# Conformer and S5 hybrid block on eight cores: first loads, DRAM casts and the convolution's steps reordered

## The reference

```python
def reference(x, meta, norm_g, w_in, b_gate, ...):
    h = jnp.concatenate([broadcast(meta), x], axis=1)     # 16 + 2048 tokens
    xn = _rmsnorm(h, norm_g)
    proj = jnp.einsum("bld,de->ble", xn, w_in)            # 2048 -> 9216
    v_c, g_c, z_c, u_s, z_s, gl_c, gl_s = _split_columns(proj)
    # mixer A: v * sigmoid(g), causal depthwise convolution of 31 taps, layernorm, silu, * silu(z)
    y_c = _conformer_conv(v_c, g_c, z_c, dw_w, dw_b, ln_g, ln_b)
    # mixer B: S5 state space scan, gelu, GLU, * silu(z)
    y_s = _s5_scan(u_s, ...)
    y_s = jax.nn.gelu(y_s)
    y_s = y_s * jax.nn.sigmoid(jnp.einsum("ble,ef->blf", y_s, w_glu) + b_glu)
    y_s = y_s * jax.nn.silu(z_s)
    merged = (jax.nn.sigmoid(gl_c + b_gate[:D_MODEL]) * jnp.einsum("ble,ed->bld", y_c, w_conv)
              + jax.nn.sigmoid(gl_s + b_gate[D_MODEL:]) * jnp.einsum("ble,ed->bld", y_s, w_ssm))
    h = h + jnp.einsum("bld,de->ble", merged, w_out)
    return _rmsnorm(h, final_g)[:, N_META:, :]
```

## Time and profile before

| | us |
|---|---|
| three timed runs, median (lowest to highest) | 1804.61 (1802.98 to 1807.88) |
| the profiled execution, its own time | 1794.7 |
| its span on the slowest core, core 5 | 1793.2 |
| spans of the eight cores | 1785.0 to 1793.2 |
| TensorE busy in that span | 1653.3 (92%) |
| VectorE, ScalarE, GpSimd busy | 738.0, 495.4, 60.9 |
| mean granted TensorE clock, all cores | 0.975 to 0.976 of 2.4 GHz |

### The profile page before, as it was taken

The page is one execution under the profiler, slowest core; times in us unless marked ns, Lnnn a source line. Parts: engine busy times, 40 slices in busy tenths (PEclk is TensorE's granted clock), DMA queues, the critical chain, the costliest instruction groups (busy, mean ns, idle before and its releaser), DMA issues.

```text
span 1793.2 us, 22788 instructions; the slowest of 8 cores (1785.0 to 1793.2 us)
## 1 busy us (share of the span) xinstructions
PE 1653.3 (92%) x8966; PEld 803.4 (45%) x8966; DVE 738.0 (41%) x1142; ACT 495.4 (28%) x700; POOL 60.9 (3%) x131
## 2 busy tenths in 40 slices
PE   1799899999999997188899999999999999999997
PEld 1344455555554443044455454444444444444443
DVE  2554488887730000245573601111221236733343
ACT  2644477777731110000131251111111100011111
POOL 1000000000000300000000000000000000000000
PEclk9999999999999999598999999999999999999999
DMA  9461022232347499700204230302221144364333
GB/s 212 143 162 42 9 72 64 70 64 67 72 96 139 58 111 111 85 16 10 33 1 71 36 60 12 59 0 40 49 51 39 46 160 165 122 229 160 141 141 117
DMA packets 33177, 149.61 MB, mean 83 GB/s; under 512 B 3936, under 2 KB 7136, under 8 KB 23648
## 3 DMA queue, kind: packets, MB, share of 16 engines
q0 software_dynamic: 13744, 60.30, 22.4%
q1 hardware_dynamic: 19328, 87.86, 13.9%
HBM read 179.07 MB, written 40.89 MB: 123 GB/s over the span
## 4 chain that ended last, share of the span: by engine, by line
PE 85%; DVE 5%; another core or an unknown queue 4%; DMA 2%; issue 2%; ACT 1%; POOL 0%; DVEq 0%; ACTq 0%; SPq 0%; POOLq 0%
PE ps L254 83%; DMA xt<-x 2%; PE ps L257 2%; DVE wc L232 1%; ACT cs L226 1%; DVE mt L232 1%; DVE xs L242 1%; DVE cs L242 0%; DVE ug L248 0%; ACT xs L228 0%; DVE g L232 0%; DVE ss L760 0%; DVE pq L232 0%; DVE ag L248 0%
## 5 line engine op out<-in xcount | busy, mean ns | idle before, releaser
L254 PE MATMUL ps<-xm,wr 128*128 128x512 bf16 x1280 | 297.4, 379 | 0.0
L254 PE MATMUL ps<-wb,xm 128*128 128x512 bf16 x1024 | 229.8, 386 | 48.9 <-DVE a L242 48.9
L254 PE MATMUL ps<-xm,zr 128*128 128x512 bf16 x1024 | 223.3, 379 | 0.0
L254 PE MATMUL ps<-wo,m 128*128 128x512 bf16 x1024 | 221.2, 379 | 0.0
L254 PEld LDWEIGHTS ps<-wb,xm 128*128 128x128 bf16 x1024 | 101.0, 100 | 172.4 <-issue 59.0
L254 PEld LDWEIGHTS ps<-xm,wr 128*128 128x128 bf16 x1280 | 119.5, 98 | 122.6 <-issue 0.2
L254 PE MATMUL ps<-xm,gr 128*128 128x512 bf16 x768 | 169.7, 379 | 0.0
L254 PEld LDWEIGHTS ps<-wo,m 128*128 128x128 bf16 x1024 | 100.2, 98 | 120.8
L254 PEld LDWEIGHTS ps<-xm,zr 128*128 128x128 bf16 x1024 | 99.6, 98 | 117.5
L254 PE MATMUL ps<-wu,xm 128*128 128x512 bf16 x512 | 120.5, 395 | 4.6 <-ACT wv L226 4.6
L228 ACT ACTIVATE jk<-h 128x2048 bf16<-128x2048 f32 x16 | 30.6, 1912 | 326.9 <-DVE h L242 326.9
(11 more groups left out here) (163 smaller groups left out, 1652.5 us busy)
## 6 DMA issues: line engine op xcount, KB each, us to landing
x<-x SPq DMA_DIRECT2D x16, 1024.0 KB, 6.9
out<-h SPq DMA_DIRECT2D x16, 1024.0 KB, 4.7
xt<-x SPq DMA_DIRECT2D x14, 1024.0 KB, 7.2
wr<-wm POOLq DMA_DIRECT2D x20, 512.0 KB, 8.6
gscr<-gst SPq DMA_DIRECT2D x20, 512.0 KB, 7.9
gr<-gscr SPq DMA_DIRECT2D x20, 512.0 KB, 3.4
wob<-wo POOLq DMA_DIRECT2D x8, 1024.0 KB, 58.6
zr<-wm POOLq DMA_DIRECT2D x16, 512.0 KB, 5.9
```

What stands on the lines that cost most here:

```text
L254: return S.op("pe", lambda e: e.matmul(out_, lhsT, rhs, start=start, stop=stop), r, w, signal=signal)
```

## The change

Six edits, in the order of the program.

**First loads.** Tiles 1 and 2 of x move from POOL's to SP's queue, tile 1 behind a wait for tile 0's landing, tile 2 behind a wait for `gf`'s. The second half of `wu` waits on POOL for tile 2's landing. `prm` moves behind them.

**Input order.** From A(i), B(i-3), T(i+2) with the norm three tiles ahead, to a written list: T0, N2, A0, T1, N3, A1 and so on, B from after T4 on. The parameter steps start at A3 instead of A1. The first scan tables are moved by a unit or two (`prep_wv(0)` before `tab_b` and `tab_c`).

**G2.** `prep_g2(q)` moves from st = 3 of q - 1 to st = 1 of q.

**DRAM casts.** The 28 casts become single instructions on POOL, each waiting for the PE unit ahead of it: seven in g1 (after units 3, 5, ... 15), eight each in v0 and v1 (odd units), five in the z part. The ten `wmb` of `wss` come first, then `wob`, then `wmb` of `wcv`. `load_wtc(0)` and `load_wtc(1)` now stand behind seven casts, not behind 28.

**Convolution.** The two copies from PSUM to `ag` go from DVE to ACT. `build_wc` is split in its two halves. `conv_tr(b + 1, 0)` moves ahead of `conv_mm(b, 1)`, `conv_tr(b, 1)` to the start of the block.

**Fillers.** One generator over all, and four places in a block instead of three: four units in each of blocks 0 to 2, eight in block 3, sixteen in blocks 4 and 5, eight in 6 and 7.

```diff
-            elif i in (1, 2):
-                dma("pool", XT[sl].ap, x_t[t], dsrc(), w=(XTb[sl],))
...
+            return dma("sp", XT[sl].ap, x_t[t], XTs[sl], w=(XTb[sl],), after=after)
...
-        load_x(0)
-        dma("sp", GF.ap, norm_g.partition_broadcast(128), dsrc(), w=(GFb,))
+        ev_x0 = load_x(0)
+        ev_gf = dma("sp", GF.ap, norm_g.partition_broadcast(128), dsrc(), w=(GFb,))
+        load_wu(0)
+        load_x(1, (ev_x0,))
+        ev_x2 = load_x(2, (ev_gf,))
         dma("sp", PRM.ap, prm_d, dsrc(), w=(PRMb,))
-        load_wu(0)
-        load_x(1)
-        load_x(2)
-        load_wu(1)
+        load_wu(1, (ev_x2,))
...
+        order = ["T0", "N2", "A0", "T1", "N3", "A1", "T2", "N4", "A2", "T3", "N5", "A3", "T4", "N6", "B0", "T5", "N7",
+                 "A4", "B1"]
+        for i in range(6, NSEQ):
+            order += [f"T{i}"] + ([f"N{i + 2}"] if i + 2 < NSEQ else []) + [f"A{i - 1}", f"B{i - 4}"]
...
-                if st == 1 and nx:
-                    tab_b(q + 1)
-                    prep_wv(q + 1)
+                if st == 1:
+                    if nx:
+                        tab_b(q + 1)
+                        prep_wv(q + 1)
+                    prep_g2(q)
...
                 if st == 3:
-                    if nx:
-                        prep_g2(q + 1)
...
+        casts = [("w", 0, i) for i in range(10)] + [("o", n, h) for n in range(4) for h in range(2)]
+        casts += [("w", 1, i) for i in range(10)]
...
+                if nb == 1 and j >= 3 and j % 2 == 1:
+                    cast((S.eng["pe"]["src"], S.eng["pe"]["src"].count))
...
-            cp("dve", AG[sl].ap[:, :, 2:130], pT.rearrange("p (g c) -> p g c", g=8), r=(PB[bk],), a=(AGb[sl],))
+            cp("act", AG[sl].ap[:, :, 2:130], pT.rearrange("p (g c) -> p g c", g=8), r=(PB[bk],), a=(AGb[sl],))
...
-            if j == 2:
-                build_wc(0)
+            if j in (2, 6):
+                build_wc(0, j // 6)
...
+        conv_tr(0, 0)
+
+        def conv_block(b, n1, n2, n3, n4):
+            conv_tr(b, 1)
             fillg(n1)
-            conv_tr(b, 1)
             conv_mm(b, 0)
+            build_wc(b + 2, 0)
             fillg(n2)
+            if b < 7:
+                conv_tr(b + 1, 0)
+            fillg(n3)
             conv_mm(b, 1)
-            fillg(n3)
-            build_wc(b + 2)
+            build_wc(b + 2, 1)
+            fillg(n4)
 
         for b in range(4):
-            conv_block(b, 1, 1, 2 if b < 3 else 1)
-        fillg(16)
-        load_z(0)
-        load_z(1)
-        gen = fill_3b()
+            if b < 3:
+                conv_block(b, 1, 1, 1, 1)
+            else:
+                conv_block(b, 2, 2, 2, 2)
         for b in range(4, 6):
-            conv_block(b, 5, 5, 6)
+            conv_block(b, 4, 4, 4, 4)
...
-            conv_block(b, 3, 2, 3)
+            conv_block(b, 2, 2, 2, 2)
```

More of the change, by code:

```diff
@@ L80, in touch, with op @@
         self.live.append(b)
-    def op(self, eng, fn, r=(), w=(), a=(), signal=True, src=None):
+    def op(self, eng, fn, r=(), w=(), a=(), signal=True, src=None, after=()):
         En = self.eng[eng]
@@ L100, in op @@
             _mx(need, b.p)
+        for ds, v in after:
+            if need.get(ds, 0) < v:
+                need[ds] = v
         kn = En["known"]
@@ L257, in tr, with dma @@
             return S.op("pe", lambda e: e.transpose(out_, in_, idn), r, w, signal=signal)
-        def dma(q, out_, in_, src, r=(), w=(), a=()):
-            return S.op(q, lambda e: e.dma_start(out=out_, in_=in_), r, w, a, src=src)
+        def dma(q, out_, in_, src, r=(), w=(), a=(), after=()):
+            return S.op(q, lambda e: e.dma_start(out=out_, in_=in_), r, w, a, src=src, after=after)
         coff = [CONST0]
@@ L338, in build, with load_x @@
         NSEQ = len(seq)
-        def load_x(i):
+        def load_x(i, after=()):
             if i >= NSEQ:
-                return
+                return None
             t = seq[i]
@@ L797, in build @@
         norm(0)
+        load_x(3)
         norm(1)
[L799 removed]
         load_x(4)
[L801 to L840 removed]
+        order = ["T0", "N2", "A0", "T1", "N3", "A1", "T2", "N4", "A2", "T3", "N5", "A3", "T4", "N6", "B0", "T5", "N7",
+                 "A4", "B1"]
@@ new lines, in build @@
+        for i in range(6, NSEQ):
+            order += [f"T{i}"] + ([f"N{i + 2}"] if i + 2 < NSEQ else []) + [f"A{i - 1}", f"B{i - 4}"]
+        order += [f"A{NSEQ - 1}"] + [f"B{i}" for i in range(NSEQ - 4, NSEQ)]
+        n_a = 0
+        for o in order:
+            i = int(o[1:])
+            if o[0] == "N":
+                norm(i)
+                load_x(i + 3)
+            elif o[0] == "T":
+                trans(i)
+            elif o[0] == "A":
+                n_a = i
+                uproj(i, 0)
+                if i >= 3:
+                    next(par, None)
+                    next(par, None)
+                if i == 10:
+                    for i_ in range(4):
+                        load_gate_w(i_)
+                if i == 14:
+                    for q in range(4):
+                        load_bc(q)
+            else:
+                uproj(i, 1)
+                if i == 8:
+                    umeta()
+                if i == NSEQ - 5:
+                    prep_wt(0)
+                    tab_a(0)
+                if i == NSEQ - 4:
+                    prep_wv(0)
+                    tab_b(0)
+                    prep_g1(0)
+                    ugt(0)
+                if i == NSEQ - 3:
+                    tab_c(0)
+                    prep_m7(0)
+                    prep_wt(1)
+                if i == NSEQ - 2:
+                    vmm(0)
+                    prep_t(0)
@@ L841, in build @@
         pump(1)
-        prep_g2(0)
         WB = [T("wb0", [128, 16, 512], BF16, D0 + 82272), T("wb1", [128, 16, 512], BF16, D0 + 32768),
@@ L941, in meta_unit, with cast @@
                     r=(PB[bk], VMb), w=(VMb,))
+        casts = [("w", 0, i) for i in range(10)] + [("o", n, h) for n in range(4) for h in range(2)]
+        casts += [("w", 1, i) for i in range(10)]
+        def cast(ev):
+            if not casts:
+                return
+            k_, p_, q_ = casts.pop(0)
+            if k_ == "o":
+                dma("pool", wo_b[p_][:, 8 * q_:8 * q_ + 8, :], wo_d[p_][:, 8 * q_:8 * q_ + 8, :], dsrc(),
+                    w=(WODb[p_][q_],), after=(ev,))
+            else:
+                dma("pool", wm_b[10 * p_ + q_], (wcv_d if p_ else wss_d)[6 + q_], dsrc(), w=(WMDb[10 * p_ + q_],),
+                    after=(ev,))
         for nb in range(2):
@@ L995, in load_wtc, with build_wc @@
                 dma("pool", WTC[b % 2].ap, wtc_d[:, 16 * b:16 * b + 16, :], WTCs[b % 2], w=(WTCb[b % 2],))
-        def build_wc(b):
+        def build_wc(b, h):
             if b >= 8:
@@ L1126, in fill_zs @@
                     load_z(i + 6)
+                for _ in range(2):
+                    cast((S.eng["pe"]["src"], S.eng["pe"]["src"].count))
         def fill_v1():
@@ L1132, in fill_3b @@
         def fill_3b():
+            yield from fill_v1()
+            load_z(0)
+            load_z(1)
             yield from fill_glu()
             yield from fill_zs()
-        gen = fill_v1()
+        gen = fill_3b()
         def fillg(n):
```

80 lines of the change are left out of this document (16 added, 64 removed).

## The result

| | before | after |
|---|---|---|
| timed runs, median (lowest to highest) | 1804.35 (1802.98 to 1807.88), 4 runs | 1733.47 (1730.50 to 1735.45), 4 runs |
| profiled execution, its own time | 1794.7 | 1730.5 |
| span of the slowest core | 1793.2 (core 5) | 1728.9 (core 1) |
| span of core 5 | 1793.2 | 1722.7 |

The ratio after to before is 0.9603, 95% interval 0.9582 to 0.9624. The change takes 71 us off. The forecast was 1706 with a range up to 1728: the time lies 27 us above the forecast and 5 above the range.

A forecast was written before the change was run, and what follows sets the result against it. TensorE, busy 92% of 1793.2 us, was held to lose time to waits in in-order queues and matmuls running long after them; input 27 + G2 4 + convolution 75 - tail 7 = 99 gained, 1804.6 to 1706; forecast 1690 to 1718, range 1690 to 1728.

The forecast's parts named there:

- The start of the input: First loads and tiles: x tiles land earlier, giving a lead of 11 us, less 3 for half-clock matmuls: 8 gained.
- The rest of the input: Input stage after 54.9 us: of 22.8 us of TensorE idling and slow matmuls, 19 gained.
- G2: Scan: moving the perm products removes 7.2 us of waits for g, less 3 of new ones: 4 gained, between 0 and 7.
- The 3 us of new waits for the bank: Scan: prep_m7 takes prep_wv's bank while ScalarE still reads it, about 0.4 us every second q, 3 in all.
- The taps: Convolution's start: TensorE's 48.9 us stall, from tap loads queued behind casts, and 1.8 of slow matmuls go: 50.7 gained.
- Rival (b): Convolution: tap loads late again, so the stall is only reduced; 1722, or 1735 with further loads late; chance 0.07.
- The convolution's order: Convolution blocks: 16.2 us of waits, 15.3 for ag and 0.9 before block 4, and 8.3 of half-clock matmuls go.
- The tail of fillers: The yc blocks, six of eight without a filler: 5.5 us of waits and 1.5 of half-clock matmuls, 7 lost, between 3 and 12.
- (a): Input: the start gives nothing since the DMA engines stay full; input gains 10 instead of 27, 1723; chance 0.14.
- (c): New small waits: longer bank waits at every q, more half-clock time at the start and yc tail; 1725; chance 0.08.
- (d): Slower than before: casts beside busy VectorE slow POOL's transfers threefold, 1829; decides from 27 us per wob; chance 0.02.

The follow-up runs named there:

- e1: The changed kernel with the second wu load and its wait moved behind consts() on POOL; timed median 1709.4 us, core 5 span 1704.6.
- e10: e1 without POOL's wait for tile 2 ahead of the second wu load; timed median 1711.4 us, core 5 span 1705.0.
- e5: e1 with the transposes and copies of ug(0) ahead of tab_b(0) and prep_g1(0); timed median 1703.6 us, core 5 span 1700.6.
- e2: The changed kernel with the first loads and input order of the kernel before; core 5 span 1722.2 us, timed median 1750.1 (includes disturbed executions).
- e8: e7 with the first five tiles' T and A in another order and tile 1's norm behind T0; timed median 1695.1 us, core 5 span 1690.4.
- e12: e7 with prep_g2 back at its old place; timed median 1697.8 us, core 5 span 1694.3.
- e3: The kernel before with only the casts and tap loads arranged as after; core 5 span 1740.8 us, timed median 1753.2 (includes disturbed executions).
- e4: The changed kernel with no casts around the convolution's start; core 5 span 1716.1 us, timed median 1744.5 (includes disturbed executions).
- e11: e7 with the convolution's steps in the old order and ag's copies on VectorE; timed median 1717.1 us, core 5 span 1711.2.
- e6: e1 with fewer fillers in convolution blocks 6 and 7, kept for the yc blocks; core 5 span 1701.8 us, timed median 1717.6 (includes disturbed executions).
- e7: The changed kernel with the four edits of e1, e4, e5 and e6 together; timed median 1695.3 us, core 5 span 1693.8.

## Why the prediction was wrong

**The start of the input (forecast 8 gained).** This is the step that failed. The working followed the transfers, and their times came out nearly: tile 1 at 21.5 (22), tile 2 at 28 (28), A0 in e1 at 26.0 (24 to 30), only its last chunk of `wu` at 32.2 and not at 28.5. The forecast took a rule from the Trainium skill, page "DMA: Bandwidth & Descriptors", section "Queues, rings and completion order": each DMA engine takes turns between the queues with work. The trace agrees for these tiles beside `wu`. What the forecast left out is what stands on GpSimd behind the wait that the change adds, though it reads every wait of the kernel before as one in an in-order queue. I read the second `wu` load's wait as a delay of `wu` alone. Behind it on GpSimd stand the iotas of `consts()`, behind these VectorE's constants, behind these the first two norms. T0 came at 40.9 instead of 18.9. e1 shows that this costs 15.0 us in the stage, e10 that it was for nothing. No row of before shows the wait; but its length could have been had from the forecast's own 28 us for tile 2, and the order of the program's text gives the rest.

**The rest of the input (forecast 19 of 22.8).** With the wait out of the way the stage ends 19.6 us before that of the kernel before (e1), and 25.9 with `ug` moved as well (e5); against e2, which has the old input in a run of its own, these are 17.3 and 23.5. The forecast for the whole stage was 27. So the missing part behind the start is the one of `ug`: I had the 4.57 us for `wv` go, rightly, and didn't ask what is late next on VectorE's queue, where `tab_b` waits for ScalarE. e5 prices this at 6.2 us (5.5 over the cores). What is left, 1 to 4 us, is of the size of the waits of 1.25 to 2.5 for a tile's own `xm` copies, which A(i) right behind T(i) brings; e8's order, which avoids some of them, gave 2.

**G2 (forecast 4, between 0 and 7): 1.5 in the result, 2.3 in e12.** Right in kind. The 3 us of new waits for the bank are 2.4 (`wv`, eight times); a second kind that I hadn't seen, for `gst`, adds 1.9.

**The taps (forecast 50.7): right.** e3 gives 51.4 for that part and 52.4 for the span. Rival (b), taps late again, didn't happen: in none of the kernels with the new casts does VectorE wait for `wtc` on core 5.

**The convolution's order (forecast 24.5): right.** From e3 (casts alone) to e4 (all, with `dwb` in time) the part falls by 19.4, and in e4 it still carries the tail's 5.4: 24.8 together, of which 1.7 is a unit that ran 5.30 behind the wait for `amt` in e3 alone. e11 gives about 18, since it keeps the new places of the fillers and so waits 12.2 for `ag` and not the forecast's 16.2; how the last 5 us divide between order and fillers I didn't test.

**The bias load (not in the forecast): 6.2 us on core 5.** The forecast said that the casts run beside tap and weight loads, and asked only whether these come in time. A third transfer, on the other queue, was the one that didn't. e4 shows it. Its size isn't steady: the wait was 4.4 in after and 4.1 in e5, but 0.6 in e1, 1.0 in e2 and none in e6 and e10, with casts in the same places. VectorE waited for the load in all of them (7.5 to 9.3). Where TensorE waited little, it had come later: the work behind its wait for `amt` ran 2.9 us long in e1, e2, e6 and e10, and not in after and e5. First e1, then after, core 5:

```profile
713.78 1.86 PE L260 MATMUL ps<-idp,a 128*128 128x128 bf16 x16 [2.66 <-DVE amt L235]
715.44 5.68 PE L257 MATMUL ps<-wb,xm 128*128 128x512 bf16 x16
```

```profile
729.05 1.05 PE L260 MATMUL ps<-idp,a 128*128 128x128 bf16 x16 [2.66 <-DVE amt L235]
729.94 3.62 PE L257 MATMUL ps<-wb,xm 128*128 128x512 bf16 x16
```

**The tail of fillers (forecast 7 lost): 5.4 (e6),** 4.0 of waits and 1.4 of slower halves; no unit behind it ran long, as I had taken 1.5 for.

**Rivals.** (a) was the nearest in kind and size: its 1723 took 10 us for the input. It came from the transfers, though, and the cause is another. (c) came in part, with `gst`; the wait for `co` is in none of the four. (d) didn't happen. The point of it was the time of a `wob`. While VectorE expands the taps, after, the DMA engines are as full and as fast with the casts (0.99, 122 GB/s) as beside the idle VectorE of the earlier trace rows (1.00, 111 GB/s), though VectorE is busy for 14.4 of 20 us; and a GpSimd issue beside its instructions on `co` takes 0.53, where eight took 4.09 in the earlier trace rows. In which mode VectorE ran no trace says, so the rule that the forecast puts behind (d) is left open. The windows view (us, PE, PEld, DVE, ACT, POOL busy, granted clock, DMA share, GB/s), then the timeline of both, core 5:

```profile
760.00:780.00 20.00, 20.00 (x148) 11.27 (x146) 14.40 (x12) 2.36 (x5) 1.55 (x3) 1.00 0.99 122
```

```profile
757.79 0.53 POOL L263 DMA_DIRECT2D wob<-wo  x1
...
757.98 1.36 DVE L235 TENSOR_TENSOR co<-ps,dwb 128x512 bf16<-128x512 f32 x2
```

**The sum.** 99 was forecast and 70.5 came. Missing were in the input 22.4 (15.0 for the wait, 6.2 for `ug`, 1.2 unplaced), in the scan 2.5, and in the convolution 3.4 net: 6.2 for `dwb`, against 2.8 that the rest did better, 1.6 of it the tail. With the three causes taken away and the tail repaired, e7 has 99.4 us less than before on core 5. It meets the 99 only because the tail, which the forecast had counted as lost, is repaired in it.

**The range.** It ended at 1728 since I let the end of rival (a) set it. An added wait that costs more than the transfer it delays had no case of its own. The 27 us by which the median missed are the 28.5 that are missing on core 5. The slowest core is another now and lies 6.2 behind core 5, at a clock of 0.987 against 0.994, which I had not allowed for; but the median lies only 4.6 above its span, where I had carried over 11.4. These two cancel by luck.

## What to carry to other kernels

An added wait is priced by the whole list of what stands behind it on its engine, down to the engines that wait for that list in turn; write the list down before looking at the transfers. A load that already stands behind another on its own queue should be tried without a wait first: here the wait bought at most 1 us (e10). When a large transfer is spread over a stretch, look at every small load of that stretch on any queue, not only at those that it was moved past.

## What the runs showed of the hardware

A load of 0.5 MB on SP's queue took 3.8 us to land with POOL's queue free (before) and 16.9 to 19.9 among DRAM-to-DRAM casts of 1 MB each on POOL's queue (e3 and after, with e1, e2, e5, e6 and e10 between them); with no cast issued for 33 us ahead of it, 4.8 and 3.4 (e4, e7). That is more than even turns would give. In the view of after, 700 to 800 us, the load is 144 packets with 2.4 us of time on each engine, 0.27 a packet, and the other queue's 1811 packets took 0.74 each. Nine packets an engine, each behind one of the other queue, would be 9 us, an estimate from these rows; the load took 19.9. What makes up the rest stayed open.

After the same 0.94 us wait for `ug`, the 16 matmuls behind it took 3.61 in e5 and 5.30 in e7, and after the same 2.66 for `amt` 3.62 in after and 5.68 in e1. The granted clock over these four units reads 1.00 and 0.67 (e5, e7), 1.00 and 0.60 (after, e1; transposes included). Whether a short wait is followed by slow matmuls isn't decided by its length alone; what else decides it stayed open. It makes the same code differ by up to 2.9 us at one place.
